# Where a hybrid block's output-gate modulation and two kept gate products stand

## The reference

```python
sh1, sc1, gt1, sh2, sc2, gt2 = modulation(c, w_mod, b_mod, 6)   # silu(c) @ w_mod + b_mod, 6 x 1024 columns
h = rmsnorm(x, g_norm1) * (1 + sc1) + sh1
k, v, a, u, q, r, hy, gates = split_cols(h @ w_in, ...)
y_gla = gla_readout(o, r)                  # bidirectional chunked attention
y_s5  = s5_readout(...)
y_hy  = x2 * long_conv(x1 * long_conv(v))  # two long convolutions, by Fourier transform
m = sigmoid(g_hy) * (y_hy @ w_hy) + sigmoid(g_gla) * (y_gla @ w_gla) + sigmoid(g_s5) * (y_s5 @ w_s5)
x = x + gt1 * (m @ w_out)
x = x + gt2 * (swiglu(rmsnorm(x) * (1 + sc2) + sh2))
out = rmsnorm(x) * g_final
```

## Time and profile before

| | us |
|---|---|
| median of 3 runs | 1220.83 (1220.79 to 1224.56) |
| profiled execution | 1218.67 |
| its span | 1216.8 |
| TensorE busy | 1112.2 (91%) |
| VectorE busy | 585.7 (48%) |
| ScalarE busy | 401.3 (33%) |
| GpSimd busy | 335.1 (28%) |

### The profile page before, as it was taken

The page is one execution under the profiler, slowest core; times in us unless marked ns, Lnnn a source line. Parts: engine busy times, 40 slices in busy tenths (PEclk is TensorE's granted clock), DMA queues, the critical chain, the costliest instruction groups (busy, mean ns, idle before and its releaser), DMA issues.

```text
span 1216.8 us, 15749 instructions
## 1 busy us (share of the span) xinstructions
PE 1112.2 (91%) x6109; PEld 848.5 (70%) x6109; DVE 585.7 (48%) x1135; ACT 401.3 (33%) x763; POOL 335.1 (28%) x288
## 2 busy tenths in 40 slices
PE   4899989978989999998997979798999999999995
PEld 1478958866567676777473654697888888888884
DVE  3775156576489888783196965435000012000014
ACT  2762323443344534432411100234332212232221
POOL 2032213503100000000131210351655545665540
PEclk9889999989889998998998989899999999999998
DMA  9920223855223323323423227661333223333211
GB/s 315 277 97 32 69 69 130 135 150 169 67 64 87 88 70 72 86 58 98 147 87 121 69 101 260 195 182 42 104 104 104 64 94 104 102 104 104 80 42 70
DMA packets 139367, 134.32 MB, mean 110 GB/s; under 512 B 12937, under 2 KB 125865, under 8 KB 138268
## 3 DMA queue, kind: packets, MB, share of 16 engines
q1 hardware_dynamic: 126448, 105.52, 29.8%
q0 software_dynamic: 3744, 16.15, 3.6%
q10 hardware_dynamic: 9100, 11.64, 3.2%
HBM read 120.18 MB, written 11.01 MB: 108 GB/s over the span
## 4 chain that ended last, share of the span: by engine, by line
PE 72%; DVE 15%; ACT 4%; issue 4%; DMA 3%; ACTq 1%; POOL 0%; DVEq 0%; SPq 0%; POOLq 0%
PE psum L744 59%; DMA buf<-in_w_mod 2%; PE psum L1077 2%; PE psum L777 1%; PE psum L1004 1%; PE psum L1107 1%; PE psum L984 1%; DMA buf<-in_w_out 1%; PE psum L789 1%; DVE ring_lo L2054 1%; PE psum L882 1%; PE psum L808 1%; PE psum L997 1%; ACTq L1580 1%; DVE buf L2130 1%
## 5 line engine op out<-in xcount | busy, mean ns | idle before, releaser
L1296 POOL TENSOR_TENSOR ring_lo<-buf,ring_hi 128x512 fp32r<-128x512 f32 (+2 forms) x220 | 281.9, 1314 | 498.0 <-ACT ring_hi L1451 497.9
L744 PE MATMUL psum<-hT_hi,ring_hi 128*128 128x512 f32 x712 | 286.7, 403 | 8.7 <-DVE hT_lo L2393 4.0
L744 PE MATMUL psum<-hT_lo,ring_hi 128*128 128x512 f32 x712 | 279.9, 393 | 0.0
L744 PE MATMUL psum<-hT_hi,ring_lo 128*128 128x512 f32 x712 | 279.7, 393 | 0.0
L1451 ACT ACTIVATE ring_hi<-buf 128x512 fp32r<-128x512 f32 (+1 forms) x260 | 139.6, 610 | 224.2 <-PE psum L744 160.8
L744 PE MATMUL psum<-buf,buf 128*128 128x512 f32 (+1 forms) x368 | 153.5, 574 | 21.4 <-issue 15.4
L744 PEld LDWEIGHTS psum<-hT_hi,ring_hi 128*128 128x128 f32 x712 | 135.5, 190 | 42.6 <-issue 5.5
L744 PEld LDWEIGHTS psum<-hT_lo,ring_hi 128*128 128x128 f32 x712 | 135.9, 191 | 28.6 <-issue 1.7
L744 PEld LDWEIGHTS psum<-hT_hi,ring_lo 128*128 128x128 f32 x712 | 135.3, 190 | 29.1
L744 PEld LDWEIGHTS psum<-buf,buf 128*128 128x128 f32 x368 | 69.4, 208 | 94.3 <-issue 85.0
L2402 DVE TENSOR_TENSOR buf<-psum,buf 128x512 f32<-128x512 f32 x22 | 15.2, 692 | 220.7 <-PE psum L744 220.7
(11 more groups left out here) (333 smaller groups left out, 1705.8 us busy)
## 6 DMA issues: line engine op xcount, KB each, us to landing
buf<-in_w_in SPq DMA_DIRECT2D x26, 1024.0 KB, 5.3
buf<-in_w_mod SPq DMA_DIRECT2D x24, 1024.0 KB, 8.3
buf<-in_w_ffn_in SPq DMA_DIRECT2D x44, 512.0 KB, 5.2
buf<-in_w_ffn_out SPq DMA_DIRECT2D x8, 1024.0 KB, 5.1
scr_k<-buf POOLq DMA_DIRECT2D x4, 1024.0 KB, 5.5
buf<-scr_k POOLq DMA_DIRECT2D x4, 1024.0 KB, 7.9
buf<-in_w_out SPq DMA_DIRECT2D x4, 1024.0 KB, 6.6
buf<-in_w_ffn_out SPq DMA_DIRECT2D x4, 768.0 KB, 4.6
```

The costliest lines, as they stand in the source:

```text
L744: ins = nc.tensor.matmul(o, a, b, start=start and n == 0, stop=stop and n == len(pairs) - 1)
L1296: nc.gpsimd.tensor_tensor(ring_lo[:, a:a + n], ring[:, a:a + n], ring_hi[:, h + i * n:h + i * n + n].bitcast(fp32), SUB)\
```

## The change

It moves two kinds of step.

- Gate products g00 and g01 (block `gate00`), which stood beside the S5 loop at the head of the kept list, now stand in the attention stage, behind `gla_exp 1` and modulation blocks 12 and 17. Their two sigmoids have buffers of their own (`sig_early`) and a semaphore of their own. The rest of the kept list moves up: beside the S5 loop are now g02 to g05, and in the convolutions g06 and g07 alone, so each later gate of branch 2 comes two places earlier.
- The eight output-gate modulation blocks no longer stand behind branch and output products. Blocks 8 to 11 stand beside the first convolution, 20 to 22 beside the second, 23 behind b01. Their rows have a place each (`gate_row`), since they are now kept until their `gt` step, which stays in the tail: 8 behind b02, 9 and 10 behind b03, 11 behind b04, 20 behind b05, 21 to 23 behind the split of m. Nothing stands between the output products any more. The gates' bias vectors have a semaphore of their own.

The order beside the convolutions is now: b20; b21, g06, g07, g22, b22, g23, mod 8, b23, mod 9, 10, 11, `yinv`, g24; then b24, g25, mod 20, b25, g26, b26, g27, b27, mod 21, `yinv`, mod 22.

```diff
         step("gla_exp", 1)
         mods(12, 17)
+        want("gate00", block(w_in, G0))
+        step("merge_g", 0, 0, 0)
+        step("gate_spill", 0, 0)
         step("gla_states", 1)
+        step("merge_g", 0, 0, 1)
+        step("gate_spill", 0, 1)
         mods_T(12, 17)
...
-        kept, ms0 = kept[0::2], kept[1::2]
+        kept, ms0 = kept[4::2], kept[1::2]
...
-        beside = [ms[1], ms[3]] + kept[4:6] + ms[4:8] + kept[6:8] + ms[8:]
+        beside = [ms[1], ms[3]] + kept[4:6] + ms[4:]
...
+        gates = [8, 9, 10, 11, 20, 21, 22, 23]
+
+        def mod_gate():
+            i = gates.pop(0)
+            want(f"mod{i}", block(w_mod, 256 * i), split=False)
+            step("mod", i)
+
         for cv in range(2):
...
             step("ufold", cv)
             one_beside()
+            if cv:
+                mod_gate()
             for jt in range(2):
                 step("uhalf", cv, jt)
...
                 step("ucomb", cv, jt)
+            if cv == 0:
+                mod_gate()
             step("uunfold", cv)
             one_beside()
+            for _ in range((3, 1)[cv]):
+                mod_gate()
             step("yinv", cv)
+            if cv:
+                mod_gate()
             one_beside()
...
+        rows_at = {2: (8,), 3: (9, 10), 4: (11,), 5: (20,)}
         for n in range(8):
             one_beside()
-            if n > 2:
+            if n == 1:
                 mod_gate()
+            for i in rows_at.get(n, ()):
+                step("gt", i)
         one_beside()
         step("mT_split")
+        for i in (21, 22, 23):
+            step("gt", i)
         for i in range(4):
             want(f"wo{i}", block(I["w_out"][0], 256 * i))
             step("wo", i)
-            mod_gate()
             if i == 0:
                 step("A2")
-        while made:
-            mod_gate()
...
             def gate_spill(b, j):
                 o = full(act, f"g{b}{j}")
-                dst = sig_free()
-                users.append((f"spilt{j % 2}", 16 * (j // 2 + 1)))
+                done = "spilt_early" if j < 2 else f"spilt{j % 2}"
+                if j < 2:
+                    dst = sig_early[j]
+                else:
+                    dst = sig_free()
+                    users.append((done, 16 * (j // 2)))
                 A(dst, o, ACT.Sigmoid).then_inc(freed(f"g{b}{j}"), 1)
...
                 o = full(dve, f"mr{i}")
-                V.tensor_copy(mrow8[i] if i < 8 else mrow[i % 2], o[:, 0:256]).then_inc(freed(f"mr{i}"), 1)
...
+                row = mrow8[i] if i < 8 else gate_row[i] if i in gate_row else mrow[i % 2]
+                V.tensor_copy(row, o[:, 0:256]).then_inc(freed(f"mr{i}"), 1)
```

More of the change, by code:

```diff
@@ L209, in hybrid_block @@
         arow = v3(r.take(256)[0:32, :], 2)
+        sig_early = [r.take(L) for _ in range(2)]
         r = Region(F + KD * L, par_at)
@@ L293, in hybrid_block @@
         y_s5 = v3(at_words(U_at, 4 * L), 4)
+        gate_row = dict(zip((8, 9, 10, 11, 20, 21, 22, 23),
+                            mrow + [restart[:, k:k + 256] for k in (0, 256, 512)]
+                            + [at_words(par_at + 512 + 256 * k, 256) for k in range(3)]))
         G5 = oT
@@ L591, in hybrid_block @@
             one_beside()
-        gates = [8, 9, 10, 11, 20, 21, 22, 23]
-        made = []
-        def mod_gate():
-            if gates:
-                i = gates.pop(0)
-                want(f"mod{i}", block(w_mod, 256 * i), split=False)
-                step("mod", i)
-                made.append(i)
-            if len(made) > 1 or not gates:
-                step("gt", made.pop(0))
         beside = ms0
+        rows_at = {2: (8,), 3: (9, 10), 4: (11,), 5: (20,)}
         for n in range(8):
             one_beside()
-            if n > 2:
+            if n == 1:
                 mod_gate()
+            for i in rows_at.get(n, ()):
+                step("gt", i)
         one_beside()
         step("mT_split")
+        for i in (21, 22, 23):
+            step("gt", i)
         for i in range(4):
@@ L798, in gt_rows @@
                 o = open_job(name)
-                close(nc.tensor.matmul(o[:, 0:256], pick[:, 0:1].to_broadcast([P, P]), mrow[i % 2],
+                close(nc.tensor.matmul(o[:, 0:256], pick[:, 0:1].to_broadcast([P, P]), gate_row[i],
                                        start=True, stop=True), name)
@@ L2354, in gt_rows @@
                 if i == 8:
[L2355 removed]
+                    dve.wait_ge(S("gate_bias"), 32)
                 name = f"gt{i}"
```

18 lines of the change are left out of this document (11 added, 7 removed).

## The result

| | before | changed |
|---|---|---|
| median, 20 runs each | 1221.31 us | 1226.97 us |
| range | 1217.32 to 1226.23 | 1220.70 to 1232.70 |
| profiled execution, its span | 1218.67, 1216.8 | 1227.28, 1225.5 |

The ratio to the kernel before is 1.004 (95% interval 1.0026 to 1.0054): slower by 0.4%, where 1215.5 was forecast. The two spans lie 8.7 us apart, the medians 5.7. One execution of the kernel before (1833 us) and one of an experiment (1842 us) ran at a granted clock of 0.56 and are in no ratio.

The account below looks back on a forecast made before the run. TensorE's chain of waits was taken as the bound, with VectorE pacing the convolutions. Terms +14.6 - 13.1 - 6.4 - 0.4 gave -5.3 us, applied to the median 1220.83: 1215.5 us, range 1210 to 1223.

Parts of the forecast that it names:

- signs named against the forecast: g00 starting in the old gap, VectorE not waiting for block 20, or long operations beside GpSimd again in the convolutions.
- Attention stage: Moved g00 and g01 delay TensorE's step from 277.36 to 292.0: +14.6 us for 10.9 us of work.
- the split's price: Attention stage: GpSimd's four pieces of g00's block take 5.6 us, so g00 starts at 265.6.
- The first convolution: Transform waits for block 11's load, then runs through; second convolution starts at 664.2 instead of 666.36: -2.2 us.
- The second convolution: VectorE waits for block 20, +7.7 us, less 4.2 of split collisions; inverse transform at 715.0 instead of 713.7.
- the price I put on block 20 alone: Second convolution: block 20's copy just before the halves costs VectorE, the pace-maker there, +7.7 us.
- The tail: w_out's load is hidden on TensorE; output products start at 761.8 instead of 774.86: -13.1 us.
- the rule's worst case: Tail merges: three operations each wait out a GpSimd piece of 1.25 us, a merge takes 6.3; sum 2.5 us less favourable.
- The output products and what follows: Four products of 11.36, 45.4 us instead of 51.85: -6.4; a last row copy of 0.43 goes too.
- The low clock through the whole of g00: Rival, attention stage: g00 takes 10.9 us at the low clock; +3.3, 1218.8 us; chance 0.22.
- The slower case: Rival: splits keep hitting VectorE's combining operations in the convolutions; +9.1 on its chain, net +3.8, 1224.6 us; chance 0.18.
- The bounds: Attention stage cost: 12 us (split 4.92, low clock 2.6 us) to 17.9 (g00 all at the low clock).

Follow-up runs that it names:

- early split: Changed kernel with block gate00's split placed ahead of the step that takes the second r half out of PSUM; median 1216.4 us, 0.9950 of the kernel before.
- attention move alone: Changed kernel with the output gates' modulation blocks put back in the tail, only g00 and g01 moved into the attention stage; 1231.3 us, 1.0073 of the kernel before.
- block 20 later: Changed kernel with modulation block 20 moved from ahead of the second convolution's halves to behind its first combination; median 1221.8 us, 0.9992 of the kernel before.
- second w_out split late: Changed kernel where ScalarE splits w_out's second block only after the first block's first output product; median 1221.5 us, 0.9998 of the kernel before.

## Why the prediction was wrong

The path was right: g00 behind GpSimd, VectorE idle for block 20, no load on the chain in the tail, four output products without gaps all came, and none of the signs named against the forecast did. It failed in the sizes of its terms and in one wait, for a PSUM bank, that it did not have. The terms, against the table:

- **Attention stage, 14.6 for 16.6: the split's price.** I took 5.6 us for it, between two rows that had other neighbours; beside VectorE's three long multiplies it took 7.71. The working also has a slip that did no harm: 290.6 and 2.5 are 293.1, not 292.0. The 2.5 counts from the first of two tiles, and the row at 272.58 holds both. From g01 to the step 6.5 us were measured and 6.6 booked. The further 2.3 (second low stretch) was in none of my terms, but as shown it comes and goes with the execution. The early split took 6.7 us out of the stage.
- **The first convolution, -2.2 for +0.9: the step "then runs through" failed.** The load's landing was right within 0.3 us. But the blocks also move g24 onto b23's bank, 1.9 us. I counted products and durations and not the bank numbers, though eight products between two uses of a bank was in the kernel's description. The rest is the low clock behind the wait, 1.3 more than booked.
- **The second convolution was right** (+3.3 for +3.5): VectorE's wait for block 20, and no collision, though the split missed VectorE in another way than I had it. What was not right is the price I put on block 20 alone, 7.7: moving it away gave 4.8, since b24's merge is next.
- **The tail was right in direction, 1.5 us short.** The wait behind b07 was 2.45 us longer than booked, because both splits come in one run (split apart, it was 3.0 us in all); the parts ahead of it were 1.0 shorter. The Trainium skill, "SBUF — State Buffer", section "Who interferes with whom", says that copies and casts, under conditions on their operands, can take the port pair shared with GpSimd too, and that the one that comes first holds it for the whole instruction. The rows agree: the cast took 1.38 for 0.43. The two merges beside the splits took 5.6 and 4.7 us, between my 4.8 and the rule's worst case of 6.3.
- **The output products and what follows, 6.8 forecast, 2.3 found: the largest miss.** I divided 51.85 us by products at the high clock, although showed the low one behind the old wait, and kept no such stretch behind the new one: 2.0 us. With the wait cut to 1.72 us the products took 45.5. The other 2.6 lie behind the products, which I had taken as unchanged.
- **The rivals.** The low clock through the whole of g00 did not come. The slower case came in sign and size (1224.6 for 1227), but by luck: no split hit the combining operations in the changed kernel. What came was a sum of misses on the same side: 2.0, 2.3, 1.4 (the S5 loop, cause open), 3.1, 1.5 and 4.5 us. The bounds, added for each stage, should have made the range wider.

## What to carry to other kernels

A product moved into a gap is free only if all its inputs are there when the gap opens: follow load, split and the engine that finishes it, and look at what else that engine's ports serve just then. Count PSUM banks and ring slots anew behind every insertion, for they set who waits for whom eight products or four loads later; here a wait for a load went from one block to another three times. Price every new wait of some 5 us or more on TensorE with the slow stretch that follows it. And compare more than one profile before a stretch at the low clock is put down to an edit: here the same steps ran with it and without it.

## What the runs showed of the hardware

- GpSimd's split and VectorE's two-input work lengthen each other: 7.71 us for 4.9 on the one side, 2.29 for 1.22 on the other. Even VectorE operations of 0.19 us took 1.19 each beside it (split early, from 256.67), about one GpSimd piece. Some single VectorE operations were held until the whole split ended (5.59 us before and in the attention move alone, 5.14 with block 20 later), others for one piece. Between 600 and 790, eight kernels show an operation held to the end for more than one piece. Each time the split directly follows GpSimd's issue of two scratch loads, and no other split there shows such a hold. No run varies this by itself, so the cause stays open.
- TensorE was granted 1.2 GHz after every idle time of 4.5 us and more that was looked at. After shorter ones the same steps gave both levels. After 3.5 us, block 11 ran in 1.93 us in the changed kernel and in 1.07 with the second w_out split late. After about 1.85 us, g00 ran at 1.00 in three kernels and fell to 0.50 two microseconds later in a fourth. The second low stretch (from about 296 on in the changed kernel) has no idle time over 2.4 us ahead of it, and is there in eight of thirteen executions, whatever the edit. What decides it is open.
- A load of 1 MB took 5.2 us in the first convolution and 12.6 in the kernel with the early split, issued behind eight scratch loads of small packets. The DMA engines moved 112 GB/s meanwhile, and 370 from 257 to 259. That the packets are the cause is argued, not tested.
